# Index scores and top-k rounds of a token block moved half a block ahead in a two-block transformer kernel

## The reference

```python
o_a = stick_breaking_attention(...)   # 4 heads of 64
o_b = nsa_attention(...)              # 8 heads: compressed, selected and window branches, gated
o_c = dsa_attention(...)              # 4 heads over the 256 keys that an indexer picks
```

## Time and profile before

| | us |
|---|---|
| Median of three runs | 3850.59 |
| The profiled execution | 3848.09 |
| Its span, first to last instruction | 3846.5 |
| Attention phase, layer 0, first reduction to the end of slot 79 | 567.88 to 794.09 |
| Attention phase, layer 1, the same | 1936.43 to 2145.79 |
| Granted clock over the span | 0.954 |

### The profile page before, as it was taken

The page is one execution under the profiler, slowest core; times in us unless marked ns, Lnnn a source line. Parts: engine busy times, 40 slices in busy tenths (PEclk is TensorE's granted clock), DMA queues, the critical chain, the costliest instruction groups (busy, mean ns, idle before and its releaser), DMA issues.

```text
span 3846.5 us, 48674 instructions
## 1 busy us (share of the span) xinstructions
PE 3700.8 (96%) x17516; PEld 2947.8 (77%) x17516; DVE 1947.0 (51%) x3253; ACT 1498.0 (39%) x2201; POOL 141.4 (4%) x133
## 2 busy tenths in 40 slices
PE   8999979999999999999889999999999998999998
PEld 6888866578888888888755688888887876878886
DVE  4443465754544344433658544443388764334433
ACT  4432244553343334422456543433233334334431
POOL 0000000000100000000000001000000001010001
PEclk9999986899999999999979999999999987989999
DMA  3223330022232222233210122223322211212231
GB/s 131 97 94 109 102 118 1 1 72 98 84 102 98 99 98 95 96 104 112 94 42 1 61 103 82 102 98 102 113 93 84 70 42 33 100 65 88 98 101 68
DMA packets 89165, 322.37 MB, mean 84 GB/s; under 512 B 10639, under 2 KB 10895, under 8 KB 89032
## 3 DMA queue, kind: packets, MB, share of 16 engines
q1 hardware_dynamic: 84384, 304.35, 23.4%
q0 software_dynamic: 3840, 13.17, 1.0%
q10 hardware_dynamic: 808, 3.07, 0.2%
HBM read 318.40 MB, written 10.02 MB: 85 GB/s over the span
## 4 chain that ended last, share of the span: by engine, by line
PE 59%; PEld 25%; issue 8%; DVE 5%; ACT 3%; PEldq 1%; POOLq 0%; DMA 0%; POOL 0%; DVEq 0%; ACTq 0%
PE bank L253 15%; PE bank L255 15%; PE bank L254 15%; PEld bank L255 8%; PEld bank L253 8%; PEld bank L254 8%; PE bank L1379 2%; PE bank L1406 2%; PE bank L847 1%; PE bank L867 1%; PE bank L838 1%; PE bank L1395 1%; DVE val L1533 1%; PE bank L877 1%; PE bank L948 1%
## 5 line engine op out<-in xcount | busy, mean ns | idle before, releaser
L249 DVE TENSOR_TENSOR unit_lo<-unit_raw,unit_hi 128x1024 fp32r<-128x1024 f32 x572 | 700.8, 1227 | 826.4 <-ACT unit_hi L244 817.7
L253 PE MATMUL bank<-h_hi,unit_hi 128*128 128x512 f32 x2688 | 1065.4, 396 | 21.8 <-DVE unit_lo L249 13.1
L254 PE MATMUL bank<-h_lo,unit_hi 128*128 128x512 f32 x2688 | 1056.8, 393 | 0.0
L255 PE MATMUL bank<-h_hi,unit_lo 128*128 128x512 f32 x2688 | 1056.2, 393 | 0.0
L244 ACT ACTIVATE unit_hi<-unit_raw 128x1024 fp32r<-128x1024 f32 x572 | 600.9, 1052 | 388.2 <-PE bank L255 375.4
L253 PEld LDWEIGHTS bank<-h_hi,unit_hi 128*128 128x128 f32 x2688 | 511.1, 190 | 133.3 <-DVE unit_lo L249 14.5
L255 PEld LDWEIGHTS bank<-h_hi,unit_lo 128*128 128x128 f32 x2688 | 511.0, 190 | 108.6
L254 PEld LDWEIGHTS bank<-h_lo,unit_hi 128*128 128x128 f32 x2688 | 511.2, 190 | 107.0 <-issue 1.7
L253 PE MATMUL bank<-act_hi,unit_hi 128*128 128x512 f32 x880 | 346.7, 394 | 0.0
L255 PE MATMUL bank<-act_hi,unit_lo 128*128 128x512 f32 x880 | 345.0, 392 | 0.0
L254 PE MATMUL bank<-act_lo,unit_hi 128*128 128x512 f32 x880 | 341.5, 388 | 0.0
(11 more groups left out here) (275 smaller groups left out, 4359.4 us busy)
## 6 DMA issues: line engine op xcount, KB each, us to landing
unit_raw<-in_units SPq DMA_DIRECT2D x572, 512.0 KB, 3.3
bias_rows<-bias_once POOLq DMA_DIRECT2D x2, 3840.0 KB, 16.7
bias_t<-bias_rows POOLq DMA_DIRECT2D x16, 256.0 KB, 3.1
x<-in_x SPq DMA_DIRECT2D x4, 512.0 KB, 7.8
out_x<-x SPq DMA_DIRECT2D x8, 256.0 KB, 2.1
mixer_gains<-in_mixer_gains ACTq DMA_DIRECT2D x2, 736.0 KB, 5.0
mixer_constants<-in_mixer_constants ACTq DMA_DIRECT2D x2, 560.0 KB, 3.8
bias_t<-bias_rows POOLq DMA_DIRECT2D x8, 128.0 KB, 2.6
```

The lines of the kernel that those rows point to most:

```text
L249: nc.vector.tensor_tensor(w_lo[u % SLOTS][:], raw[u % SLOTS][:], w_hi[u % SLOTS][:].bitcast(F32), ALU.subtract).then_inc(unit_lo, 1)
L253: nc.tensor.matmul(out_ap, w_h, r_h, start=first, stop=False)
L254: nc.tensor.matmul(out_ap, w_h, r_l, start=False, stop=False)
L255: return nc.tensor.matmul(out_ap, w_l, r_h, start=False, stop=last)
```

## The change

In the attention phase:
- Index heads of block b + 1 go from slots 14 to 17 of block b, two a slot, to slots 1 to 8, one a slot.
- Top-k rounds get a function of their own, `choose`, called after the reduction. Round i of block b + 1 is done in slot 20 b + 11 + i: rounds 0 to 8 in slots 11 to 19 of block b, rounds 9 to 15 in slots 0 to 6 of block b + 1.
- The compressed branch's steps go from slots 2, 4, 6, 8, 10, 12 to 3, 5, 7, 9, 10, 12.
- Stick-breaking: Exp goes from slot 6 to 7 (Abs stays), Ln from 7 to 8, the addition on DVE from 9 to 10, the sums from 10, 12, 14 to 11, 13, 15 and their reading to 12, 14, 16, the last Exp from 16 to 17, the product with the values from 17 to 19; its copy stays in 19.

At the end of the projection phase:
- ACT's Sigmoid of the gates goes from behind the loop to step 25; its scaling on DVE (line 724) now comes after the keys' chain.
- The keys' hidden rows are copied in step 29 instead of 30, PE makes the keys' second product behind unit 29 with a semaphore of its own, ACT copies it in step 30, DVE normalises it after the last split, and ACT's square root stands in step 31, before the Silu of the values' part.

```diff
-        pe.wait_ge(s["t_out"], 3 * TB)
+            if u == 29:
+                pe.wait_ge(s["hid"], 2)
+                for g in range(G):
+                    mm = nc.tensor.matmul(bank[2][0:NC, g * HD:(g + 1) * HD], hid[g][:, 0:NC], w2(0), start=True, stop=True)
+                mm.then_inc(s["cmp_keys"], 1)
+
         pe.wait_ge(s["hid"], 4)
-        for g in range(G):
-            mm = nc.tensor.matmul(bank[2][0:NC, g * HD:(g + 1) * HD], hid[2 * 0 + g][:, 0:NC], w2(0), start=True, stop=True)
...
+            if u == 25:
+                act.wait_ge(s["small_out"], TB)
+                sm = small[:].rearrange("p (b c) -> p b c", b=TB)
+                nc.scalar.activation(sm[:, :, GATE:GATE + 24], sm[:, :, GATE:GATE + 24], ACT.Sigmoid).then_inc(s["gates"], 1)
+            if u == 30:
+                act.wait_ge(s["cmp_keys"], 1)
+                nc.scalar.activation(kcn[0:NC, 0:P], bank[2][0:NC, 0:P], ACT.Copy).then_inc(s["zn"], 1)
+            if u == 31:
+                act.wait_ge(s["head_sum"], 13)
+                nc.scalar.activation(hstd[0:NC, 0:2], hss[0:NC, 0:2], ACT.Sqrt, bias=eps_col[0:NC, 0:1],
+                                     scale=1.0 / HD).then_inc(s["head_std"], 1)
             if u in (28, 31):
...
-            if u in (30, 31):
-                kv = u - 30
+            if u in (29, 31):
+                kv = 0 if u == 29 else 1
...
-    Z_MADE, Z_READ, SUM_MADE, SUM_READ = (0, 2, 4), (1, 3, 5), (10, 12, 14), (11, 13, 15)
-    EXP_SLOT, LN_SLOT, SP_SLOT, W_SLOT, PV_SLOT, OUT_SLOT = 6, 7, 9, 16, 17, 19
+    Z_MADE, Z_READ, SUM_MADE, SUM_READ = (0, 2, 4), (1, 3, 5), (11, 13, 15), (12, 14, 16)
+    EXP_SLOT, LN_SLOT, SP_SLOT, W_SLOT, PV_SLOT, OUT_SLOT = 6, 8, 10, 17, 19, 19
...
-        b, i = divmod(q - 14, JOBS)
-        return [(b + 1, 2 * i + e) for e in range(2)] if 0 <= b < TB - 1 and 0 <= i < 4 else []
+        b, h = divmod(q - 1, JOBS)
+        return [(b + 1, h)] if 0 <= b < TB - 1 and 0 <= h < 8 else []
+
+    ROUNDS, ROUND_FIRST = 16, 11
+
+    def top_round(q):
+
+        b, i = divmod(q - ROUND_FIRST, JOBS)
+        return (b + 1, i) if 0 <= b < TB - 1 and i < ROUNDS else None
...
-    CMP_SCORES, CMP_SHIFT, CMP_EXP, CMP_SCALE, CMP_TURN, CMP_OUT = 2, 4, 6, 8, 10, 12
+    CMP_SCORES, CMP_SHIFT, CMP_EXP, CMP_SCALE, CMP_TURN, CMP_OUT = 3, 5, 7, 9, 10, 12
...
                 nc.scalar.activation(sb_a[:], sb_z[:], ACT.Abs).then_inc(s["sb_abs"], 1)
+            elif slot == EXP_SLOT + 1:
                 act.wait_ge(s["sb_abs"], h + 1)
...
-            if b > 0 and j < 16:
-                src = index_s if j == 0 else picked
-                if j == 0:
-                    dve.wait_ge(s["idx_acc"], 8 * b)
-                link(nc.vector.max(top8[:, 0:8], src[:, 0:n]))
-                link(nc.vector.match_replace(picked[:, 0:n], top8[:, 0:8], src[:, 0:n], -3e38))
-                if j == 15:
-                    link(nc.vector.tensor_scalar(mask_k[:, 0:n], picked[:, 0:n], -2e38, NEG, ALU.is_gt, ALU.mult))
+
+        def choose(b, i):
+            n, src = (b + 1) * P, picked if i else index_s
+            if i == 0:
+                dve.wait_ge(s["idx_acc"], 8 * b)
+            link(nc.vector.max(top8[:, 0:8], src[:, 0:n]))
+            link(nc.vector.match_replace(picked[:, 0:n], top8[:, 0:8], src[:, 0:n], -3e38))
+            if i == ROUNDS - 1:
+                link(nc.vector.tensor_scalar(mask_k[:, 0:n], picked[:, 0:n], -2e38, NEG, ALU.is_gt, ALU.mult))
...
             if q < SLOTS2:
                 reduce(q)
+            if top_round(q):
+                choose(*top_round(q))
             for bh in index_heads(q - 1):
                 index_sum(*bh)
```

More of the change, by code:

```diff
@@ L217, in program @@
               "sq_summed stat_sum stat_std stat_rs stat_diag rstd h_f32 h_hi h_lo "
-              "dve_step x_val x_hi x_lo pad sb_out v_out t_out turned roped small_out hid cmp_mm cmp_turned mixer_in zn head_sum head_std gates vcb_zero "
+              "dve_step x_val x_hi x_lo pad sb_out v_out t_out turned roped small_out hid cmp_mm cmp_keys cmp_turned mixer_in zn head_sum head_std gates vcb_zero "
               "job_red job_sc job_exp job_tr job_pv pt_out ring_in ring_out o_part gate up gate_free rs_out hid_n hid_tr split_hi split_lo coef cmp_scaled sb_z sb_sp sb_c sb_w sb_o sb_d sb_zm sb_abs sb_e sb_ln idx_acc "
@@ L617, in mix1_act @@
                                          bank[5 - kv][:, g * NC:(g + 1) * NC].unsqueeze(1).to_broadcast([P, n, NC]), ACT.Copy).then_inc(s["hid"], 1)
-        act.wait_ge(s["small_out"], TB)
-        sm = small[:].rearrange("p (b c) -> p b c", b=TB)
-        nc.scalar.activation(sm[:, :, GATE:GATE + 24], sm[:, :, GATE:GATE + 24], ACT.Sigmoid).then_inc(s["gates"], 1)
+        act.wait_ge(s["vcb_zero"], 1)
         act.wait_ge(s["cmp_mm"], 1)
-        nc.scalar.activation(kcn[0:NC, 0:P], bank[2][0:NC, 0:P], ACT.Copy).then_inc(s["zn"], 1)
-        act.wait_ge(s["vcb_zero"], 1)
         for h in range(4):
@@ L626, in mix1_act @@
             nc.scalar.activation(vc_blk[rows, h * P:(h + 1) * P], bank[3][rows, 0:P], ACT.Copy)
-        act.wait_ge(s["head_sum"], 13)
-        nc.scalar.activation(hstd[0:NC, 0:2], hss[0:NC, 0:2], ACT.Sqrt, bias=eps_col[0:NC, 0:1],
-                             scale=1.0 / HD).then_inc(s["head_std"], 1)
         act.wait_ge(s["cmp_turned"], 1)
@@ L721, in mix1_dve @@
         nc.vector.memset(vc_blk[:], 0.0).then_inc(s["vcb_zero"], 1)
+        rows = slice(0, NC)
+        squares(12, kcn, rows, 2)
+        normalise(12, kcn, rows, 2, gn[0:NC, 1152:1280], cos_c[0:NC, :], sin_c[0:NC, :]).then_inc(s["roped"], 1)
         dve.wait_ge(s["gates"], 1)
@@ L724, in mix1_dve @@
         nc.vector.tensor_scalar(sm[:, :, GATE + 24:GATE + 32], sm[:, :, GATE + 24:GATE + 32], float(np.float32(8 ** -0.5)), float(np.float32(32 ** -0.5)), ALU.mult, ALU.mult)
-        rows = slice(0, NC)
-        squares(12, kcn, rows, 2)
-        normalise(12, kcn, rows, 2, gn[0:NC, 1152:1280], cos_c[0:NC, :], sin_c[0:NC, :]).then_inc(s["roped"], 1)
     JOBS, BATCHES = 20, 5
```

## The result

| | before | after |
|---|---|---|
| Median of the runs side by side, us | 3850.69 (4 runs, 3847.55 to 3863.12) | 3905.48 (4 runs, 3894.91 to 3914.29) |
| The profiled execution | 3848.09 | 3913.97 |
| Its span | 3846.5 | 3912.4 |
| Attention phase, layers 0 and 1 | 226.2 and 209.4 | 233.2 and 243.8 |
| Granted clock over the span | 0.954 | 0.938 |

The ratio is 1.0144, with an interval of 1.0116 to 1.0172: slower by 1.4%, where I had forecast 3837 and a range that ended at 3864. Rival C named the place, but its 3863 is 42 us short.

A forecast was written before the change was run, and what follows sets the result against it. PE bounds the weight stages; in attention DVE bounds slots 0 to 9, PE 10 to 19. From 3848.1, attention gains 10 (37.6 less 28 for low clock), projections' end 4; plus 2.5 for the median: 3837, range 3815 to 3864.

The forecast's parts named there:

- Rival C: Attention's first halves: low clock makes PE slow with lone heads at about 1.6 to 2 us; 3863; chance 0.19.
- I put half of today's 133 us, 66, at 0.42: Attention, both layers: low-clock time falls from 133 to 66 us, each costing 0.42 us, 28 us in all.
- the rule of the prediction: Attention stage: low time counted as 2 x (1 - granted clock) x the stretch's length.
- its own sign: Slots 0 to 9 of block 1 at clock 0.50 in both layers would show the low-clock rival.
- Rival A: Attention: PE filled in both halves keeps the clock, 20 us low time instead of 66; 3817; chance 0.14.
- Rival B: Attention's first halves: PE and DVE lock at equal loads, losing 3 to 4 us a half; 3849; chance 0.24.
- The index price: Index products on PE: a lone head costs 0.63, 0.84 or 1.05 us, 20.2 us a layer against 13.1.
- The halves: Attention's half blocks added up at full clock: 199 us a layer, 398 for two against 435.6.
- 1.3 us there for nine rounds on DVE: Second half of attention block 0: nine top-k rounds on DVE add 1.3 us, within a half of 20.
- No idle before the stick-breaking product: Attention's second halves: PE no longer waits for ACT's weights before this product, 0.7 us less each.
- The projections' end: Tail after the last weight unit: work taken off ACT's chain gains 2 us a layer, 4 in all.

The follow-up runs named there:

- e2: Kernel before with only the attention phase changed, the projections' end as before: 3916.4 us, ratio 1.0156.
- e3: Kernel before with only the index heads moved to slots 1 to 8, one a slot: 3913.0 us, ratio 1.0101.
- e7: Changed kernel with each index product over all 128 rows, scores summed over four heads, so not the reference's result: 3853.3 us, ratio 0.9976.
- e10: Changed kernel with index products over 128 rows, each head's queries copied by GpSimd into a tile of zeros: 3852.3 us, ratio 1.0001.
- e12: e10 with head 0's stick-breaking operations in the slots of the kernel before: 3856.9 us, ratio 0.9995.
- e6: Kernel before with only the index heads and top-k rounds moved as in the change: 3892.3 us, ratio 1.0090.

## Why the prediction was wrong

- **The step that failed** is the sentence "I put half of today's 133 us, 66, at 0.42". By the rule of the prediction, low time outside block 0's first half is 82 us in layer 0 and 108 in layer 1, 190 together. The halves had been added up to 398 at full clock and took 477.1, so 79 us for 190, again 0.42 a us. With 190 in place of 66 the sum is 3886. That the price fits so well is in part luck: the 79 us also hold waits in the second half of block 0 (below). The rest to 3914 of the profiled execution lies outside the attention phases, 11 of it ahead of layer 0's.
- The reason given for the half was that fuller halves keep the clock. After, e2, e3 and e7 show the opposite for this filling: PE was busy 36.89 of 36.89 us at 0.64 with products on 32 rows (after), and with products on 128 at the same places it was busy 24.80 of 26.33 at 1.00 (e7). Between after and e7 nothing differs but how many rows the index products use and, by that, which scores come out; e10 has the right scores and the same clock.
- **Rival C** had the mechanism: PE-bound first halves at low clock, lone heads at 1.6 and 2.0 us (measured 2.0 at 512 keys), decided at 99 us (190 came). By its own sign, 0.50 in block 1's first half in both layers, it did not come: these halves stood at 0.64 and 0.70, as they begin at full clock. And its price was low, but not in those halves. It put 46 us on the first halves of blocks 1 and 2 in both layers; they came out 28.5 over my sum. What it left out are the second halves of blocks 0 to 2: 28.9 and 28.8, 27.8 and 27.2, 32.9 and 37.3 us against my 20, 23.5 and 27, which is 42 us over. I gave it 0.19; the profile before had already shown 33.76 of 33.76 us busy at 0.62, and that row should have weighed more.
- **Rival A**, the clock kept, is refuted, and with it the use of the rule cited there. The Trainium skill ("TensorE: Matmul & The Clock Gate", section What's actually happening) says that activity releases the throttle; here PE was busy 36.89 of 36.89 us and the clock fell in the midst of them, to a mean of 0.64, as in the row that spoke against it in the prediction.
- **Rival B**, engines that lock: e10 has both at equal loads and full clock, 24.79 and 24.70 us busy in a half of 26.32, and 20.53 and 20.43 in 23.00. The loss is 1.5 to 2.5 us, as the forecast had it, and not 3 to 4.
- **The index price** was right at full clock: 0.84 and 1.05 us a product with 384 and 512 keys in after itself, as put. The layer's 33.7 against 20.2 is clock. e10's 23.3 (layer 1) is over the 20.2 because the first products of block 0 ran at the low clock, 1.15 us or more against the 0.63 put for 256 keys.
- **The halves**, tested by e10: blocks 1 to 3 were put at 158 us and take 157.4 in layer 1. That is partly luck: the second halves of blocks 1 and 2 take 27.0 (at 0.88) and 28.5 (at 1.00) against 23.5 and 27, and the other four are shorter than put. Block 0 was put at 41 and takes 51.2. In its second half PE now waits for DVE's subtractions and weights, which stand behind the rounds. I had put 1.3 us there for nine rounds on DVE, by load and not by order. With the stick-breaking slots of before it goes back: 23.4 us in e12, 23.9 and 24.3 in e6. This is the second term that failed, about 9 us a layer in after, clock and wait together.
- **No idle before the stick-breaking product** came true: the ACT wait of the earlier trace rows is gone. In its place these waits of layer 1 have grown; before they were 0.6, 1.0 and 0.6 us (who waited for whom, us, times, longest):

```profile
PE bank L952 <- DVE sb_z L1114: 4.6, 4, 1.6
PEld bank L890 <- DVE coef L1155: 4.0, 2, 2.4
PE bank L890 <- DVE coef L1155: 3.6, 2, 2.3
```

- **The projections' end**: put at 2 us a layer, 2 to 3 by the starts above. ACT in time order, answering to the earlier trace rows:

```profile
565.58 1.28 ACT L623 ACT_TABLE_LOAD   x1
567.36 0.42 ACT L623 ACTIVATE zn<-bank 32x128 f32<-32x128 f32 x2 [0.50 <-PE bank L530]
...
569.43 1.11 ACT L635 ACTIVATE vc_blk<-bank 32x128 f32<-32x128 f32 x4 [0.81 <-PE bank L552]
570.55 0.20 ACT L637 ACTIVATE kc_t<-bank 128x32 f32<-128x32 f32 x1
```

  From the last Silu to the key copy are 3.2 us instead of 7.4. That Silu ends its wait for PE, not for its table.

## What to carry to other kernels

Before work is moved into a stretch, read that stretch's granted clock and price the work at it; if the engine that gets it is TensorE, ask which rows of the array the work uses, and compare with a run in which it uses all. That was the cure here, and not a rule: the spell at 527.5 us was low with 128 rows at work. A stage that another engine bounds hides a low clock, and the hiding ends when TensorE gets its load. A profile of one execution can stand at either end of its spread, as before's did outside the attention phases (short) and in layer 0's (long): compare it with others before a difference in unchanged code is explained.

## What the runs showed that I had not expected

- TensorE, busy all of 35 to 42 us, had a mean clock of 0.56 to 0.65 where the added products used 32 rows, and the fall came inside a stretch in which it never idled; with 128 rows, three quarters of them zeros, the clock was 0.98 to 1.00, and some 50 us of the kernel's 3905 came back.
- More rows at work for the same result made the kernel faster: 1.0001 (e10) against 1.0144.
- The kernel before varied by 1.3% (3831 to 3882) over 94 runs, with low spells in unchanged code that cost about 12 us and come or stay away.
- 24 copies of 32x128 a layer on GpSimd, 0.29 to 0.36 us each, hid beside attention work: PE waited for none of them.
